# Inverting the diagonal blocks of the delta rule in 32s instead of 16s, with decay factors from cumulative sums

## What is computed

```python
decay = jnp.cumsum(g, axis=-1)
gamma = jnp.exp(jnp.where(causal, decay[..., :, None] - decay[..., None, :], -jnp.inf))
a_mat = jnp.where(strict, jnp.einsum('bhnid,bhnjd->bhnij', kb, k) * gamma, 0.0)
sol = lax.linalg.triangular_solve(a_mat + eye, rhs, left_side=True, lower=True)
```

## Time and profile before

| | us |
|---|---|
| median of 3 runs | 1528.21 (1526.46 to 1528.42) |
| profiled execution, its own time | 1527.25 |
| its span | 1525.4 |
| TensorE busy | 1485.3 (97%) |
| VectorE busy | 1039.8 (68%) |
| ScalarE busy | 589.6 (39%) |
| GpSimd busy | 378.9 (25%) |

### The profile page before, as it was taken

One profiled execution on the slowest core, in us unless ns is written; L12 is line 12 of the kernel. 1 busy time (PEld: TensorE's weight loads), 2 busy tenths in 40 slices (PEclk: granted clock), 3 DMA queues, 4 the chain that ended last, 5 costly groups with the idle time before them and its releaser, 6 DMA issues.

```text
span 1525.4 us, 26665 instructions
## 1 busy us (share of the span) xinstructions
PE 1485.3 (97%) x9756; PEld 915.0 (60%) x9756; DVE 1039.8 (68%) x2031; ACT 589.6 (39%) x1241; POOL 378.9 (25%) x465
## 2 busy tenths in 40 slices
PE   7999999999999999999999999999998999999997
PEld 6455885444444466677676676655445787854443
DVE  3639999999996566766776766545834676747434
ACT  4538321111111546556556455333113666621111
POOL 0130124322330224403404303001101454456000
PEclk9999999999999999999999999999999999999999
DMA  9310223233312311211211212335664000055132
GB/s 373 94 57 1 73 79 119 89 110 104 117 55 86 85 31 55 81 47 44 72 43 57 71 31 84 104 95 181 218 218 141 23 22 29 16 194 194 54 111 83
DMA packets 132156, 142.69 MB, mean 94 GB/s; under 512 B 16746, under 2 KB 105298, under 8 KB 130388
## 3 DMA queue, kind: packets, MB, share of 16 engines
q1 hardware_dynamic: 119828, 120.27, 24.8%
q10 hardware_dynamic: 12096, 20.98, 3.8%
q0 software_dynamic: 128, 0.03, 0.0%
HBM read 110.18 MB, written 31.08 MB: 93 GB/s over the span
## 4 chain that ended last, share of the span: by engine, by line
PE 59%; DVE 3%; ACT 3%; POOL 2%; issue 1%; DMA 0%; SPq 0%; DVEq 0%; POOLq 0%; ACTq 0%
PE ps L92 14%; PE ps L93 14%; PE ps L94 14%; PE ps L1927 2%; PE ps L1509 1%; PE ps L1412 1%; PE ps L1476 1%; PE ps L1470 1%; PE ps L1464 1%; DVE g_o L1261 1%; PE ps L1450 1%; PE ps L1404 1%; PE ps L1530 1%; PE ps L1458 1%; PE ps L1514 1%
## 5 line engine op out<-in xcount | busy, mean ns | idle before, releaser
L92 PE MATMUL ps<-g_h_hi,g_piece_hi 128*128 128x512 f16 x544 | 207.0, 381 | 2.6 <-PEq L2117 2.6
L93 PE MATMUL ps<-g_h_lo,g_piece_hi 128*128 128x512 f16 x544 | 206.9, 380 | 0.0
L94 PE MATMUL ps<-g_h_hi,g_piece_lo 128*128 128x512 f16 x544 | 206.8, 380 | 0.0
L92 PE MATMUL ps<-g_h_hi,a_w_hi 128*128 128x512 f16 x448 | 169.9, 379 | 3.1 <-DVE g_h_lo L565 2.4
L94 PE MATMUL ps<-g_h_hi,a_w_lo 128*128 128x512 f16 x448 | 169.8, 379 | 0.0
L93 PE MATMUL ps<-g_h_lo,a_w_hi 128*128 128x512 f16 x448 | 169.8, 379 | 0.0
L655 DVE MATCH_REPLACE8 a_ada<-a_best,a_ada 128x1024 f32<-128x1024 f32 (+2 forms) x192 | 167.7, 886 | 0.0
L652 DVE MAX8 a_best<-a_ada 128x8 f32<-128x1024 f32 (+2 forms) x192 | 162.0, 891 | 0.7 <-DVE a_ada L641 0.3
L897 POOL TENSOR_TENSOR g_shared<-g_shared 128x120 f32<-128x120 f32 (+14 forms) x120 | 54.0, 450 | 244.9 <-DMA g_shared<-diagonal_blocks 234.6
L497 ACT ACTIVATE a_x<-ps 128x512 f32<-128x512 f32 x48 | 28.7, 597 | 196.5 <-PE ps L94 196.4
L92 PE MATMUL ps<-g_o,g_h_hi 128*128 128x128 f16 (+1 forms) x416 | 100.0, 268 | 1.0 <-DVE l_b L2048 0.9
(11 more groups left out here) (329 smaller groups left out, 3551.0 us busy)
## 6 DMA issues: line engine op xcount, KB each, us to landing
a_w<-in_w_in SPq DMA_DIRECT2D x17, 1024.0 KB, 5.8
g_piece<-in_w_in SPq DMA_DIRECT2D x34, 512.0 KB, 3.7
channel_gates<-a_x ACTq DMA_DIRECT2D x48, 256.0 KB, 2.0
g_shared<-diagonal_blocks SPq DMA_DIRECT2D x32, 256.0 KB
a_ada<-in_w_ada ACTq DMA_DIRECT2D x4, 1024.0 KB, 9.5
a_x<-in_x SPq DMA_DIRECT2D x8, 512.0 KB, 8.6
delta_gate<-a_x ACTq DMA_DIRECT2D x32, 128.0 KB, 1.8
g_shared<-delta_gate SPq DMA_DIRECT2D x8, 512.0 KB, 3.9
```

The source lines that it names most:

```text
L92: pe.matmul(out, a_hi, b_hi, start=first, stop=False)
L93: pe.matmul(out, a_hi, b_lo, start=False, stop=False)
L94: return pe.matmul(out, a_lo, b_hi, start=False, stop=last)
```

## The change

The inverse of the diagonal blocks starts from blocks of 32. GpSimd substitutes 31 steps instead of 15, on 8 x 31, 8 x 30, ... 8 elements per partition. The table of blocks is now 4 MB per head and does not fit: it is cut into eight tables of 4 rows each (512 KB), which go through the two halves of `lb`; from the third on SP issues a table's load when GpSimd has used up the one that lay there. The second half of `lb` also holds `span`. The product scratch `tmp` moves into `sq_junk`, and so `square_q` waits for the end of the substitution (`base_ok`). On TensorE the level from 16 to 32 is gone (`middle16`, `outer16`), and with it VectorE's flips, mask product and subtraction; `expand` moves from slot 31 to 36.

The decay factors: the front stage also stores the cumulative sums, transposed, in DRAM (one more matmul, two copies, two small transfers). In the delta stage SP loads the row of a head into all partitions at slot 23 (`row_load`, 512 KB, behind `base_ok`), GpSimd subtracts the column sums and adds the mask (two passes of 1024 elements instead of one), and ScalarE takes one exponential at slot 12 instead of two at 10 and 11. TensorE's `decay` is gone.

```diff
@@ constants
-K_ID, K_UPTO, K_AFTER, K_ONES, K_BLOCK, K_PAIR, K_UNIT = 0, 128, 256, 384, 512, 640, 704
+K_ID, K_UPTO, K_AFTER, K_ONES, K_BLOCK, K_UNIT = 0, 128, 256, 384, 512, 640
@@ phase_front, TensorE
+            nc.tensor.matmul(g.ps[0:NT * H, 6 * BANK + 384:7 * BANK], g.g[:].rearrange("p i h -> p (i h)"), g.const[:, K_UPTO:K_UPTO + P],
+                             start=True, stop=True).then_inc(sums_mm, 1)
@@ phase_front, ScalarE
+            nc.scalar.copy(g.csum[:], totals[:, 0])
+            nc.scalar.copy(sum_rows[:], g.ps[0:NT * H, 6 * BANK + 384:7 * BANK]).then_inc(sum_rows_ok, 1)
...
+            act.dma_start(g.csum_dram, sum_rows[:]).then_inc(sum_rows_out, 16)
@@ phase_delta, names
-BASE = 16
+BASE = 32
+BLOCKS = P // BASE
+CHUNK = 4
...
+        tmp = sq_junk[:].rearrange("p t n -> p (t n)").bitcast(F32)
@@ SP, diagonal(h)
-                for b in range(NT if h else NT // 2):
+                for b in range(BLOCKS if h else BLOCKS // 2):
                     rows = slice(b * BASE, (b + 1) * BASE)
                     sp.dma_start(g.diag_dram[b], a_t[h % 2][rows, :, rows]).then_inc(diag_out, 16)
...
-                sp.wait_ge(gam_mm, 2 * h + 2)
-                if h:
-                    sp.wait_ge(xm, 3 * h - 2)
-                each = BASE * NT * BASE // 4
-                for n in range(4):
-                    sp.dma_start(lb[:, n * each:(n + 1) * each],
-                                 bass.AP(g.diag_dram.tensor, n * each, [[4 * each, NT], [0, BASE], [1, each]])).then_inc(lb_in[n], 16)
+                sp.wait_ge(gam_ok, 2 * h + 2)
+                each = CHUNK * NT * BASE
+                for n in range(BASE // CHUNK):
+                    if n >= 2:
+                        sp.wait_ge(sub, (2 * BASE - 1) * h + 1 + 2 * CHUNK * (n - 1))
+                    sp.dma_start(lb[:, n % 2 * each:(n % 2 + 1) * each],
+                                 bass.AP(g.diag_dram.tensor, n * each, [[BASE * NT * BASE, BLOCKS], [0, BASE], [1, each]])).then_inc(lb_in[n % 4], 16)
+
+            def row_load(h):
                 if h:
+                    sp.wait_ge(base_ok, h)
+                sp.dma_start(lb[:, T:2 * T], bass.AP(g.by_head_dram.tensor, h * T, [[0, P], [1, T]])).then_inc(row_in, 16)
@@ GpSimd, substitute(h) and spans(h)
-                    if j % 4 == 0:
-                        pool.wait_ge(lb_in[j // 4], 16 * (h + 1))
+                    if j % CHUNK == 0:
+                        n = j // CHUNK
+                        pool.wait_ge(lb_in[n % 4], 16 * (2 * h + n // 4 + 1))
...
-                nc.gpsimd.tensor_tensor(span, g.const[:, K_AFTER:K_AFTER + P].unsqueeze(1).broadcast_to(shape),
-                                        g.g[:, :, h:h + 1].broadcast_to(shape), ALU.mult).then_inc(span_ok, 1)
+                pool.wait_ge(row_in, 16 * (h + 1))
+                nc.gpsimd.tensor_tensor(span, span, g.csum[:, :, h:h + 1].broadcast_to(shape), ALU.subtract).then_inc(span_ok, 1)
...
+                nc.gpsimd.tensor_tensor(span, span, unseen.unsqueeze(1).broadcast_to(shape), ALU.add).then_inc(span_ok, 1)
@@ ScalarE, decay(h) and square_q(h, half)
+                act.wait_ge(span_ok, 2 * h + 2)
                 if h:
-                    act.wait_ge(attn_ok, 2 * (h - 1) + half + 1)
-                nc.scalar.activation(gam[:, 4 * half:4 * half + 4], tiles(4 + half), ACT.Exp).then_inc(gam_ok, 1)
+                    act.wait_ge(attn_ok, 2 * h)
+                nc.scalar.activation(gam, span, ACT.Exp).then_inc(gam_ok, 2)
...
                 act.wait_ge(sqk, 2 * h + 2)
+                act.wait_ge(base_ok, h + 1)
@@ TensorE
-            def decay(h, half):
...
-                mm(tiles(4 + half), ident_b[:], future[:].unsqueeze(1).broadcast_to([P, 4, P]), start=True, stop=False, skip_group_check=True)
-                for t in range(4):
-                    last = mm(at(4 + half, t), span[:, 4 * half + t], upto, start=False, stop=(t == 3), skip_group_check=True)
...
-            def middle16(h):
...
-            def outer16(h):
```

More of the change, by code:

```diff
@@ L68, in constant_table @@
     t[:, K_CAUSAL:K_CAUSAL + P] = np.where(col > row, BELOW, 0)
[L69 to L73, removed]
+    t[:, K_BLOCK:K_BLOCK + P] = row // 32 == col // 32
+    t[:, K_UNIT:K_UNIT + 32] = row % 32 == np.arange(32)[None, :]
     return t
@@ L831, in _ @@
                     diagonal(slot // SLOTS)
+                if slot % SLOTS == 23 and slot // SLOTS + 1 < H:
+                    row_load(slot // SLOTS + 1)
                 if slot % 4 == 3 and 2 * QUERY <= slot // 4 < 2 * LATENT:
@@ L921, in _ @@
                     pool.wait_ge(at_ok, NT)
-                    for b in range(NT // 2, NT):
+                    for b in range(BLOCKS // 2, BLOCKS):
                         rows = slice(b * BASE, (b + 1) * BASE)
@@ L1068, in _ @@
                         square_q(h, u - 30)
-                    if u in (10, 11):
-                        decay(h, u - 10)
+                    if u == 12:
+                        decay(h)
                     if u in (100, 101):
@@ L1191, in expand @@
                     dve.wait_ge(tr[(h - 3) % 2], before(h - 3, 8) + 8)
-                if h:
-                    dve.wait_ge(xm, 3 * h - 2)
-                for odd in range(2):
-                    nc.vector.transpose(flip[:, :, odd], pairs[odd]).then_inc(turned, 1)
-                shape = [P, NT, NT, BASE]
+                shape = [P, NT, BLOCKS, BASE]
                 nc.vector.tensor_tensor(t2[:, h % 3].rearrange("p t (b i) -> p t b i", i=BASE), tc.unsqueeze(2).broadcast_to(shape),
@@ L1394, in project @@
                     last.then_inc(proj, 1)
-            def decay(h, half):
-                if h == 0:
-                    pe.wait_ge(consts, 1)
-                else:
-                    pe.wait_ge(attn_ok, 2 * (h - 1) + half + 1)
-                pe.wait_ge(span_ok, h + 1)
-                mm(tiles(4 + half), ident_b[:], future[:].unsqueeze(1).broadcast_to([P, 4, P]), start=True, stop=False, skip_group_check=True)
-                for t in range(4):
-                    last = mm(at(4 + half, t), span[:, 4 * half + t], upto, start=False, stop=(t == 3), skip_group_check=True)
-                last.then_inc(gam_mm, 1)
             def products(h, half):
                 pe.wait_ge(silu, 3 * h + 1)
-                pe.wait_ge(gam_ok, 2 * h + half + 1)
+                if h:
+                    pe.wait_ge(attn_ok, 2 * (h - 1) + half + 1)
                 for t in range(4):
@@ L1451, in scores, with middle32 @@
                 last.then_inc(qk, 1)
-            def middle16(h):
-                pe.wait_ge(flip_ok, 3 * h + 1)
+            def middle32(h):
+                pe.wait_ge(flip_ok, 2 * h + 1)
                 if h:
                     pe.wait_ge(x_ok, 2 * h)
-                for i in range(NT):
-                    last = mm(half_at(2, i), a_t[h % 2][:, i], flip16[:, i], start=True, stop=True)
-                last.then_inc(xm, 1)
-            def outer16(h):
-                pe.wait_ge(x16_ok, h + 1)
-                for i in range(NT):
-                    last = mm(half_at(3, i), x16[:, i], columns(t2[:, h % 3, i], 16, 1), start=True, stop=True)
-                last.then_inc(tx, 1)
-            def middle32(h):
-                pe.wait_ge(flip_ok, 3 * h + 2)
                 for i in range(NT):
@@ L1474, in outer32 @@
                 pe.wait_ge(x_ok, 2 * h + 1)
+                pe.wait_ge(pad, 3 + h)
                 for i in range(NT):
@@ L1553, in _ @@
                             products(h, half)
-                        if u == 10:
-                            decay(h, half)
                     if u == 44:
```

99 lines of the change are left out of this document (40 added, 59 removed).

## The result

The changed kernel takes 1778.68 us in the median of four runs (1774.09 to 1779.55); the kernel before, beside it, 1527.4 (1526.46 to 1528.42). The ratio is 1.164, with a 95% interval of 1.162 to 1.166: 16% slower where 12% was forecast. The profiled execution took 1779.18 us, 64 more than the 1715 of the sum.

A forecast was written before the change was run, and what follows sets the result against it. TensorE's queue bounds the kernel before; then GpSimd's substitution, slowed by table loads, stops TensorE each head. The profiled time was 1276.8 + 8x, with x = 54.8: 1715, so 1716 us, 12% slower; range 1625 to 1780.

The forecast's parts named there:

- matmuls of the decay: On TensorE, the two halves of the decay leave the queue: 2.2 us per head.
- A: Moment in each head when VectorE ends the system matrix; forecast at 516.4 us for head 0.
- x: Per head, time from the first table load's issue to the substitution's end: 54.8 us, bounds 50.7 to 60.
- restarts: From B to the next A: 20.4 us in head 0, then 21.0; thin covers could add 0 to 3 in seven.
- signs named: In the trace: 80 us period, TensorE idle 20 to 25, ScalarE waiting for GpSimd, table waits, 0.62 us steps, DMA share near 0.25.
- four engines: Table loads with outermost dimension four use four DMA engines: 93 GB/s, 5.6 us per 512 KB.
- first rival: Table loads use all engines, 1.4 us per transfer; x 40.0 with hits from VectorE, time 1597 us; chance 0.13.
- B: Moment in each head when GpSimd's substitution ends, x after the first table load's issue.
- cover over the weight load: Slot 22's weight, queued on SP behind the last table, lands about B − 1: just hidden, 0 to 3 us.
- second rival: Weight lands 5 us after B; ScalarE's cast of slot 28 sets S: +40 us, 1755; chance 0.12.
- S: Moment when TensorE starts a head's scores, behind ScalarE's squares, 2.3 us after B; head 7 at 695.1 + 8x.
- decay chain: Row load, two GpSimd passes and exponential end at B + 10.6, needed at B + 15: hidden; if late, 0 to 3 us per head.

The follow-up runs named there:

- all three edits: Changed kernel with products written over the table, slot 22's weight load from ScalarE's queue and table loads over 16 engines (also spelled all_three): 1599.92 us, ratio 1.048.
- the early row: all three edits plus the ring's halves swapped and the row load issued when table 6 is used up, not at the substitution's end: 1587.69 us, ratio 1.040.

## Why the prediction was right, and what it missed

**The direction and the mechanism.** TensorE was the bound, the substitution's end became it, and TensorE stops once per head. The path from the substitution's end to TensorE was the forecast one, the scores behind the squares, in head 0 alone; in the seven others it led over the late weight. The matmuls of the decay paid as forecast (16.7 us for 8 x 2.2); no run takes out the 16-wide products alone. The step from A to the first issue came at 3.9 us, as worked out.

**How near it was.** The measured 1778.68 us lies 1.3 us inside the upper end of the stated range, 1625 to 1780. The prediction's own bounds, added up, end at 1757 + 7 x 3 = 1778, not at the 1775 that it gives. Two terms erred the same way, and x of 59.1 stayed under its bound of 60 while the restarts went past theirs (4.4 to 5.2 us over in heads 3 to 6, where at most 3 was allowed). The direction and the cause were worked out; that the range still holds the result is in part luck. Of the signs named, the waits for tables (seven of eight a head), the step of 0.62 us and the DMA share came true. The period is 88 to 89 us from A to A in the late heads where 80 was said, TensorE's stretch in head 4 is 30 us and not 20 to 25, and ScalarE waits for the weight, not for GpSimd.

**The four engines.** Shown: the DMA share is 0.27 at 86 GB/s in the changed kernel and 0.82 at 205 GB/s with the outermost dimension 32, and x falls by 17.4 us. The first rival was 0.13 and is out, and the run shows what it would have been: x 41.7 for the 40.0 worked out. The Trainium skill (DMA: Bandwidth & Descriptors, Why a DMA increments its semaphore by 16 and not by 1) has a transfer use the largest number of engines up to 16 that divides both slowest dimensions; the trace agrees, with shares of 0.27, 0.46 and 0.82 for outermost dimensions of 4, 8 and 32.

**x, mis-sized by 4.3 us.** 54.8 was forecast; the mean of the eight heads is 59.1, 34.5 us in all. In head 4, with 59.45: from issue to first product 9.7 us, not 7.6 (1.4 + 5.6 + 0.6); later waits for tables 14.4, not 11.0; the arithmetic 35.4, not 36.2. The error is the load's pace. At 93 GB/s I had it steady from 1.4 us on; the 9 us of the first window move at 86 GB/s. The upper bound, 6.4 us per transfer and x = 58.8, from the rate of the old table loads, was the better value. The old loads, like the new, read the same rows again and again, and that may be why; no run separates this from the length of the rows.

**The cover over the weight load failed.** It was costed at nothing and given 0 to 3 us, with the landing at B − 1. In head 4 it was issued at B − 10.2 and landed at B − 0.2, 0.8 us later than worked out, and ScalarE's squares start at B + 1.9, so on that path the cover was as thin as said. The step that failed is what was queued behind it. I had listed only ScalarE's squares and so the scores; I had not followed `al_ok`, from ScalarE's copy through VectorE to the second half of `turn_q`. TensorE therefore stopped two slots earlier, in heads 3 to 7. Nor had I followed VectorE's half of the weight to the recurrence step, where TensorE stopped in heads 1 and 2. From B to the next A it is 20.9, 21.6 and 22.5 us in the first three heads, where 20.4 and 21.0 were worked out, and 25.4 to 26.2 in the next four: 21.6 us over seven restarts, and 6.5 more before the last scores. The second rival had the place right (ScalarE's cast of slot 28 sets S) and the condition wrong: it did not take a weight 5 us after B. The run with the weight on ScalarE's queue removes that wait and 32 us.

**The sum.** S of head 7 is at 1198.39, forecast 1133.5. The 64.9 us are: 1.0 from the first A, 1.3 from the stores, 34.5 from x, 21.6 from the restarts, 6.5 from the last B to S. What follows S was forecast within 0.9 us. So one mechanism was missed, the chain over `al_ok`, for some 26 us (heads 3 to 7), and one size, the pace of the loads, for 34; both have the same sign.

**The covers that held.** The decay chain: row load to pass 4.4 us, two passes, exponential; no wait of TensorE or VectorE on it in the changed kernel, where the next A comes at B + 25. The exponential ends at B + 19.6 in head 4, not at the B + 10.6 worked out, since other work of ScalarE stands ahead of it. The chain came to light only when the rest was gone: with all three edits the next A comes at B + 16, and the early row brings it to B + 13.

## What to carry to other kernels

Before a transfer is made larger and issued in a ring, look at its outermost dimension: here 4 instead of 32 cost 137 us, and the trace shows it as a DMA share of a quarter while the table loads are in flight. When a queue gets waits, list all that stands behind them on that queue, and for each of these follow who waits for the engine that it stops, head by head, to the end of the chain; the second and third in line were what was missed. And run the parts of a change alone: one part of this one was a gain of 1% hidden in a loss of 16%.

## What the runs showed of the hardware

**GpSimd is held up by VectorE instruction by instruction.** In all_three each of the eight stretched GpSimd instructions of head 5, 0.3 to 0.6 us by their size, took 1.2 to 1.8 us beside a VectorE instruction with two long operands in SBUF. So it is for all 60 instructions in that run's substitutions that took over 1 us, and for all 26 in the changed kernel. I had counted four hits of 1.05 from the earlier trace rows, and the changed kernel has three or four in seven heads; that the number grows once VectorE is free I had not expected. The Trainium skill (SBUF — State Buffer, SBUF: two separate sides) describes a port pair that VectorE and GpSimd hold in turn for a whole instruction; the trace agrees, in 60 of 60 and 26 of 26. It goes the other way too: VectorE's convolution takes 1543 ns in the mean in the changed kernel, 1290 before. Of the 60 convolutions of the changed kernel, those that ran without a GpSimd instruction beside them took 1277 ns in the mean, and the longest three, beside GpSimd's passes over 1024 elements, 3.4 us.
